# A float32 output projection whose late half becomes three products of rounded parts, in a fused two-block decoder layer stack on one core

## The reference, cut to what matters

```python
# first block, mixer 1
x = x + jnp.concatenate([y_a, y_b], axis=-1) @ w_out[l]
h = rms_norm(x, ffn_norm_g[l]).reshape(Bsz * S, D)
x = x + hier_moe(h, ...)
# second block, layer 0 (mixer 2) and layer 1 (HGRN2)
oa = rms_norm_2(oa, ret_g) * jax.nn.silu(heads(ag, RET_HEADS))
o = jnp.concatenate([oa.reshape(b, t, -1), ob.reshape(b, t, -1)], axis=-1)
h = h + o.astype(h.dtype) @ w_out          # 256 x 1024 times 1024 x 1024
h = h + swiglu(rms_norm_2(h, norm_ffn_g[l]), ...)
...
o = rms_norm_2(o, norm_g) * jax.nn.silu(heads(g))
h = h + o.reshape(b, t, d) @ w_out
h = h + moe_swiglu(rms_norm_2(h, norm_ffn_g[l]), ...)
```

## Time and profile before

| | |
|---|---|
| median of 3 runs (lowest, highest) | 2070.43 us (2069.76, 2073.31) |
| the profiled execution: its time, its span | 2070.48 us, 2068.7 us |
| TensorE busy, weight loads | 93% of the span, 58% |
| VectorE, ScalarE, GpSimd busy | 31%, 22%, 3% |
| chain that ended last, by engine | TensorE 70%, DMA 19%, VectorE 7%, ScalarE 2% |
| DMA | 653.16 MB, 316 GB/s over the span, 420 to 425 GB/s in the mixtures |
| float32 late and early halves of the projections (line 771) | 87.9 us, 3% of the chain |

### The profile page before, as it was taken

One profiled execution on the slowest core, in us unless ns is written; L12 is line 12 of the kernel. 1 busy time (PEld: TensorE's weight loads), 2 busy tenths in 40 slices (PEclk: granted clock), 3 DMA queues, 4 the chain that ended last, 5 costly groups with the idle time before them and its releaser, 6 DMA issues.

```text
span 2068.7 us, 38186 instructions
## 1 busy us (share of the span) xinstructions
PE 1923.2 (93%) x16861; PEld 1204.1 (58%) x16861; DVE 642.0 (31%) x1167; ACT 465.3 (22%) x652; POOL 70.1 (3%) x30
## 2 busy tenths in 40 slices
PE   9989978677887999999999999999999998999997
PEld 8988634343433898999999864433333433333433
DVE  4872311111111973644585640010010010010011
ACT  4621201100111553543465320100000010000011
POOL 5420000000000000000000000000000000000000
PEclk9999988988888999999999999999999999999999
DMA  8253699999999641555643358999999999999996
GB/s 321 100 204 122 267 422 424 425 425 422 425 424 392 234 149 35 163 186 191 236 161 125 123 200 344 388 422 420 421 420 420 420 419 422 420 421 417 409 419 270
DMA packets 126704, 653.16 MB, mean 316 GB/s; under 512 B 8928, under 2 KB 31584, under 8 KB 81376
## 3 DMA queue, kind: packets, MB, share of 16 engines
q1 hardware_dynamic: 126560, 650.98, 78.4%
HBM read 649.90 MB, written 1.05 MB: 315 GB/s over the span
## 4 chain that ended last, share of the span: by engine, by line
PE 70%; DMA 19%; DVE 7%; ACT 2%; issue 1%; SPq 0%; DVEq 0%; ACTq 0%
PE psum L2152 18%; DMA ring<-in_w_gate 15%; PE psum L2217 7%; PE psum L2158 6%; PE psum L579 5%; PE psum L581 5%; PE psum L580 5%; PE psum L1761 4%; PE psum L771 3%; PE psum L2222 3%; DMA ring<-in_moe_w_gate 2%; PE psum L2524 2%; DMA ring<-in_moe_w_down 1%; DVE arena L1219 1%; PE psum L628 1%
## 5 line engine op out<-in xcount | busy, mean ns | idle before, releaser
L2152 PE MATMUL psum<-ring,arena 128*32 128x384 f32 (+1 forms) x3584 | 366.8, 540 | 3.0 <-DMA ring<-in_moe_w_gate 1.8
L581 PE MATMUL psum<-ring_r 128*128 128x256 f32 x944 | 266.6, 282 | 0.0
L2152 PEld LDWEIGHTS psum<-ring,arena 128*32 128x32 f32 x3584 | 117.2, 110 | 214.9 <-issue 209.6
L1761 PE MATMUL psum<-ring,arena 128*32 128x512 f32 x896 | 153.6, 755 | 60.2 <-DMA ring<-in_w_gate 59.0
L2217 PE MATMUL psum<-ring,arena 128*32 128x512 f32 x1600 | 198.2, 594 | 9.5 <-DMA ring<-in_moe_w_down 9.4
L581 PEld LDWEIGHTS psum<-ring_r 128*128 128x128 f32 x944 | 180.4, 191 | 0.0
L579 PE MATMUL psum<-ring_r 128*128 128x256 f32 x608 | 176.8, 291 | 2.7 <-DVE ring_r L659 2.6
L580 PE MATMUL psum<-ring_r 128*128 128x256 f32 x608 | 172.7, 284 | 0.0
L2398 DVE TENSOR_TENSOR arena<-arena,psum 128x512 f32<-128x512 f32 (+1 forms) x42 | 23.7, 617 | 384.0 <-issue 348.0
L1761 PEld LDWEIGHTS psum<-ring,arena 128*32 128x32 f32 x896 | 39.8, 134 | 167.3 <-issue 167.3
L2158 PE MATMUL psum<-ring,arena 128*32 128x512 f32 (+1 forms) x1120 | 131.6, 539 | 0.0
(11 more groups left out here) (462 smaller groups left out, 2802.3 us busy)
## 6 DMA issues: line engine op xcount, KB each, us to landing
ring<-in_w_gate SPq DMA_DIRECT2D x64, 1024.0 KB, 21.7
ring<-in_moe_w_gate SPq DMA_DIRECT2D x64, 1024.0 KB, 20.1
ring<-in_moe_w_down SPq DMA_DIRECT2D x32, 2048.0 KB, 20.1
ring<-in_w_up SPq DMA_DIRECT2D x48, 1024.0 KB, 25.4
ring<-in_w_down SPq DMA_DIRECT2D x24, 2048.0 KB, 25.7
ring<-in_moe_w_up SPq DMA_DIRECT2D x48, 1024.0 KB, 20.8
ring<-in_moe_w_gate SPq DMA_DIRECT2D x64, 768.0 KB, 18.5
ring<-in_moe_w_up SPq DMA_DIRECT2D x48, 768.0 KB, 18.4
```

The lines of the kernel that those rows point to most:

```text
L581: return nc.tensor.matmul(out, al, bh, start=False, stop=stop, **kw)
L1761: mm = nc.tensor.matmul(bank(0)[s * C:(s + 1) * C, :], q_Xg[:, k * PC + x * C:k * PC + (x + 1) * C], w[s][:, k, :], start=(k == 0), stop=( ...
L2152: mm = nc.tensor.matmul(bank(b0 + j)[n * MORE:(n + 1) * MORE, 0:Q], z_Xg[:, x:x + MORE], w[:, (2 * h + j) * Q:(2 * h + j + 1) * Q], start= ...
```

## The change

- `late_products` takes the place of the late blocks. A quarter is 16 products of the rounded and the remainder weights by the rounded `y` and then 8 of the rounded weights by the remainder of `y`: 24 fp32r products for 8 float32 ones. The first 16 wait for the rounded `y` and the remainder weights of quarter 0, quarter 1 for the other remainder weights.
- ScalarE rounds the late four chunks of the output weight into slot 6, quarter by quarter (`out_weights_hi`, four activations of 128 x 1024 for each projection), after the last input projection has been through that slot. VectorE writes the remainders over the weights (`out_weights_lo`, four subtractions).
- `split_y` makes `y` in two parts in slot 5: rounded, full, remainder. The gate is multiplied in ahead of the wait for rstd.
- In HGRN2 the warm-up in front of the late half is 9 matmuls, not 12.
- Since slots 5 and 6 stay in use until the end of the projection, up 0 and down 1 of moe1 are sent after it. For moe2 `SLOT_ORDER` puts slot 4 ahead of slot 6; chunk 7 alone is sent after the last input projection, chunks 8, 9, 10 after quarter 1 and chunks 6, 11, 12, 13 after quarter 3.

```diff
-SLOT_ORDER = (1, 2, 3, 5, 6, 4, 0)
+SLOT_ORDER = (1, 2, 3, 5, 4, 6, 0)
...
+        def out_weights_hi(act, st, part, tag, last, late, quarters=range(4)):
+            act.wait_ge(*E[st].at(f"{last}_q3"))
+            for r in quarters:
+                w, landed_sem, value = piece(part, f"{tag}_{r // 2}")
+                act.wait_ge(landed_sem, value)
+                nc.scalar.activation(out_hi[st][:, r], late_columns(w, late, r), ACT.Copy).then_inc(*S[st].step())
...
+        def split_y(dve, st, y, rstd, hi, lo, name):
+            v = V[st]
+            nc.vector.tensor_tensor(hi, y, rstd, ALU.mult).then_inc(*v.step())
+            v.name(f"{name}_hi")
+            nc.vector.tensor_tensor(y, y, rstd, ALU.mult).then_inc(*v.step())
+            dve.wait_ge(*v.last())
+            nc.vector.tensor_tensor(lo, y, hi.bitcast(F32), ALU.subtract).then_inc(*v.step())
+            v.name(f"{name}_lo")
...
+            def late_products(self, r, late, tokens, first):
+                for b in (2 * r, 2 * r + 1):
...
+                    for k in range(4):
+                        for w in (out_hi[self.st][:, r, b % 2, k, :], lo[:, k, :])[0:2 if first else 1]:
+                            mm = nc.tensor.matmul(bank(r)[:, (b % 2) * T:(b % 2 + 1) * T], w, tokens[:, k, :],
+                                                  start=False, stop=(not first and k == 3), skip_group_check=True)
...
-                self.pe.wait_ge(*ready)
-                for b in range(8):
-                    mm = self.block(b, late, False)
...
+                self.pe.wait_ge(*V[self.st].at(f"{self.tag}_lo0"))
+                self.pe.wait_ge(*y_hi)
+                for r in range(4):
+                    if r == 1:
+                        self.pe.wait_ge(*V[self.st].at(f"{self.tag}_lo3"))
+                    self.late_products(r, late, hi, True)
+                    if r == 0:
+                        self.pe.wait_ge(*y_lo)
+                    self.late_products(r, late, lo, False).then_inc(*E[self.st].step())
...
+                    if r:
+                        following(r - 1)
...
-            out.finish(v.at("h1y"), lambda r: route_quarter(pe, M2, r), warm=12)
+            out.finish(v.at("h1y1_hi"), v.at("h1y1_lo"), lambda r: route_quarter(pe, M2, r), warm=9)
...
+            sp.wait_ge(*piece_used("hg1"))
+            moe2_load(0, 7)
+            sp.wait_ge(*E["hgrn"].at("out3_0_1"))
+            for at in (8, 9, 10):
+                moe2_load(0, at)
+            sp.wait_ge(*E["hgrn"].at("out3_1_1"))
+            for at in (6, 11, 12, 13):
+                moe2_load(0, at)
```

More of the change, by code:

```diff
@@ L410, in _ @@
             send_down(one(0), 0)
[L411 to L414, removed]
+            sp.wait_ge(*piece_used(last_in("one", 2)))
+            for half in range(2):
+                send_ups(one(2), half, 0, 1)
+            sp.wait_ge(*piece_used(last_in("one", 3)))
+            for half in range(2):
+                send_ups(one(0), half, 0, 0)
+            send_down(one(1), 2)
+            for half in range(2):
+                send_ups(one(3), half, 1, 1)
             sp.wait_ge(*V["route1"].at("trips"))
@@ L1135, in mixer1_scalar @@
             s.name("wT")
+            out_weights_hi(act, st, "one", "out1", "z", 4)
             act.wait_ge(*e.at(f"o{NCH - 1}"))
@@ L1360, in mixer1_vector @@
                     dve.wait_ge(*v.last())
-            dve.wait_ge(*s.at("o_rstd"))
[L1363 to L1367, removed]
+            out_weights_lo(dve, st, "one", "out1", 4, range(4))
+            dve.wait_ge(*s.at("o_sq"))
+            yb = m1_ycat[:, HC:2 * HC]
+            nc.vector.scalar_tensor_tensor(yb, bank(6, 2), param("dn_g"), m1_sz, ALU.mult, ALU.mult).then_inc(*v.step())
+            dve.wait_ge(*v.last())
+            dve.wait_ge(*s.at("o_rstd"))
+            split_y(dve, st, yb, m1_X, yh_r, yl_r, "y")
             M1.router_times_gamma(dve)
@@ L2727, in attend_tensor, with attend_vector @@
             sums(1)
-        def attend_vector(dve, x, decay, meanwhile=None, between=lambda c: None):
+        def attend_vector(dve, x, decay, meanwhile=None, between=lambda c: None, last=False):
             e, s, v, tag = E[x.st], S[x.st], V[x.st], x.tag
@@ L2748, in attend_vector @@
                 meanwhile()
+            if last:
+                for t in range(NT):
+                    y = by_time(x.y, t)
+                    dve.wait_ge(*s.at(f"{tag}osq{t}"))
+                    dve.wait_ge(*s.at(tag + "gate"))
+                    nc.vector.scalar_tensor_tensor(y, bank_heads(6 + t), x.gain, by_time(x.gate, t), ALU.mult, ALU.mult)\
+                        .then_inc(*v.step())
+                    dve.wait_ge(*v.last())
+                    dve.wait_ge(*s.at(f"{tag}orstd{t}"))
+                    split_y(dve, x.st, y, by_time(c_AT, t), by_time(yh_r, t), by_time(yl_r, t), f"{tag}y{t}")
+                v.name(tag + "y")
+                return
             for t in range(NT):
@@ L2918, in mixer2_tensor @@
             attend_tensor(pe, RET, out, (1, 1, 1, 0, 1))
-            out.finish(v.at("ay"), lambda r: norm_tensor(pe, "ffn", r))
+            out.finish(v.at("ay1_hi"), v.at("ay1_lo"), lambda r: norm_tensor(pe, "ffn", r))
         def mixer2_scalar(act, waits):
@@ L3001, in mixer2_scalar @@
             keep("ag", halves(a_gate), parts=(1,))
+            out_weights_hi(act, st, "two", "out2", "ag", 0, (0, 1))
             for b in range(2):
@@ L3010, in mixer2_scalar @@
             s.name("akd")
+            out_weights_hi(act, st, "two", "out2", "ag", 0, (2, 3))
             act.wait_ge(*s.at("ag_1"))
@@ L3142, in mixer2_vector @@
             v.name("aqd")
-            attend_vector(dve, RET, lambda h, c: CHUNK_DECAY[h])
+            out2_lo = ((0, 1), (), (2, 3))
+            attend_vector(dve, RET, lambda h, c: CHUNK_DECAY[h],
+                          between=lambda c: out_weights_lo(dve, st, "two", "out2", 0, out2_lo[c]), last=True)
             for n in range(2):
@@ L3626, in hgrn_vector @@
                 gated_vector_round(dve, HG[1], n)
-            attend_vector(dve, HG[1], decay)
+            attend_vector(dve, HG[1], decay,
+                          between=lambda c: out_weights_lo(dve, st, "two", "out3", 4, range(4) if c == 2 else ()),
+                          last=True)
             M2.router_times_gamma(dve)
```

41 lines of the change are left out of this document (27 added, 14 removed).

## The result

The changed kernel takes 2075.47 us in the median of 20 runs (2072.53 to 2080.61), the kernel before 2071.97 in 20 runs beside it (2069.76 to 2074.90): a ratio of 1.0017, 95% interval 1.0011 to 1.0023. The forecast was 2064.5, range 2061.5 to 2070.5. So the change costs some 3.5 us where 6 were to be saved. The profiled execution took 2073.07 us, with a span of 2071.2, 2.5 above the span of before. What follows is read from these two executions and so accounts for 2.5 of the 3.5 us.

The account below looks back on a forecast made before the run. Mixtures bound by DMA (moe2 also TensorE) end as much earlier as they start; stretches between are TensorE's. Savings 2.3 + 0.6 + 3.1 = 6.0 us off 2070.48 give 2064.5; own range 2061.5 to 2066.5, 8 in 10 2061.5 to 2070.5.

Parts of the forecast that it names:

- The price of a quarter: Late output projections: 24 fp32r products at 0.120 us replace 16 instructions at 0.216, 3.45 to 2.88 us, 0.57 saved.
- rival 2: Late quarters: weight loads of 0.19 us not overlapped, so 24 products take 4.6 us; 2082.4 us in all, chance 0.04.
- Mixer 1, "I cost these at nothing": Mixer 1's weight rounding and subtractions fit engine waiting time, y is not waited for, so 2.3 us are saved.
- Mixer 2: Mixer 2's projection: residual sum waits for ffn weight remainders, so net only 0.6 us saved (ends 0.4 and 1.1).
- The stand of 2.1 us before the norm: Mixer 2: TensorE idles 2.1 us before quarter 0's norm matmul, which comes 0.5 later, at 828.5.
- If one overruns it costs 0.1 us: Mixer 2: added roundings and subtractions fit narrowly in ScalarE's 2.05 and VectorE's 2.46 us gaps; an overrun costs 0.1 us.
- HGRN2: Last mixer's projection: late half starts 0.8 us earlier and four quarters save 2.3, together 3.1 us.
- The held-back loads: Moved moe1 and moe2 loads land before the first buffer release, margins 6 and 1 us, so nothing is lost.
- Rival 1: Prefetch late at the first release, costing up to 9.9 us in moe1 and 7.5 in moe2: 2081.9 us, chance 0.08.
- 1.3 us to start: Held-back loads: 1.3 us allowed for the first load to start, in the landing times 221.1 (moe1) and 1223.0 (moe2).
- side estimate: Before moe2: at the skill's 358 GB/s limit chunks would land at 1227, costing some 2 us; not charged.
- Rival 3: VectorE replaces TensorE at more ends than mixer 2, or the clock halves (3.4 us): about 2067.7 us, chance 0.22.

Follow-up runs that it names:

- e4: The kernel before with only mixer 1's output projection and the moe1 loads changed: 2077.17 us, ratio 1.0019.
- e1: The kernel before with seven one-element VectorE memsets added at the end of mixer 1, nothing of the change: 2078.51 us against 2072.60, ratio 1.0033.
- e2: The changed kernel with VectorE's final_g scalings moved behind the z bias and bv's remainders: 2069.86 us, ratio to the kernel before 0.9987.
- e9: The changed kernel with SyncE holding the load of av until mixer 2's softplus is done: 2075.89 us, ratio to the kernel before 1.0018.
- e5: The kernel before with only mixer 2's output projection changed, all loads as before: 2073.63 us, ratio 1.0007.
- e7: The changed kernel with final_g scalings behind the z bias, mixer 2's weights rounded after the decayed keys, residual sums between feed-forward remainders: 2065.66 us, ratio to before 0.9970.
- e3: The kernel before with only the last mixer's output projection and the moe2 loads changed: 2068.90 us, ratio 0.9982.

## Why the prediction was wrong, point by point

- **The price of a quarter** was right: 3.13 us for a train of 24 with its last end, so 0.12 a product, and rival 2 (weight loads set the pace) is out.
- **Mixer 1, "I cost these at nothing"** is the step that failed. The cover was there, as forecast: the late half waits for neither weights nor `y`, and moe1 starts 2.66 us earlier against 2.3. But the four subtractions and the three-step `y` were priced by their duration alone. As instructions they also moved the border of VectorE's code by seven places in the program, 500 us further on, from where nobody waits to just ahead of bv's remainders. That cost 5.2 us in the changed kernel, 5.2 in e4, and 5.4 with seven empty instructions in e1. That the border had lain well in before was luck: no part of the working looked at it.
- **Mixer 2** was forecast at -0.6 and lost 2.1 from the mask on (228.2 against 226.1). The stand of 2.1 us before the norm came as forecast and is paid for in the -0.6. "If one overruns it costs 0.1 us" was mis-sized: ScalarE began 1.83 us late, and TensorE waited 0.95. The half clock behind the stand (0.72 over 831 to 836) was left out of the sum; its 3.41 us cost about 1.7, an estimate at half speed. With -0.5 these make the 2.1. An instruction packet runs just where ScalarE stands (796.47 to 797.02), so this may be ScalarE's code. For it: e2 and e9 stand at the same place (1.78 and 2.03 us), as in the changed kernel behind 459 of ScalarE's records and 1.0 to 1.2 us after a packet, and e5, with five records fewer ahead of its roundings, does not. No run was made to test it. Alone, without ScalarE's stand, the part gave -0.5 (e5), and with both repairs -2.7 (e7), of the 2.3 us that four quarters of products can give and what the sums' order adds.
- **HGRN2** was right: 3.0 against 3.1. In e3 the last two stages are 2.5 us shorter and the median 3.7, in a kernel whose clock stays whole in mixer 3, as in before.
- **The held-back loads** were right. The DMA engines were busy until about the first release of moe2, as the thin margin of 1 us had it, and moe2 got no longer (857.6 against 859.2). Rival 1 is out. The forecast's 1.3 us to start is not in its rows; in the changed kernel the first packets ahead of moe2 move 0.95 us after the issue (1204.71 and 1205.66). Its side estimate, chunks in at 1227, lies 3.1 us behind the 1223.9 and not some 2; the sum did not use it.
- **Rival 3** had a new VectorE wait and a half clock take the gain, and both happened, at more than twice its price. The half clock behind mixer 2's stand is one that it named; the wait at bv's remainders and the half clock there, the larger loss, are not. No rival slower than before rested on VectorE.

The Trainium skill (Runtime: NRT & Kernel Launch, Instruction fetch mechanics) says that an engine's instructions come in blocks of 16 KiB, 256 instructions, each fetched while the one before runs, so that a border is mostly hidden. The trace does not agree for this border: 2.5 to 3.25 us in the open in six kernels. The same section of the Trainium skill warns that a taken branch can force such a fetch. VectorE leaves the loop of moe1 ahead of this place, but no run here shows whether that is why.

## What to carry to other kernels

Count instructions, not only their time: here seven more on VectorE shifted the place where, as far as the runs tell, its code is loaded, and that cost 5 us, some 500 us behind the edit. When an engine stands and the named semaphore was already given, look for an instruction packet in the DMA view, and test by adding a few empty instructions to the old kernel. If it is so, put work that nobody waits for at the border, as e2 did, before giving up the change.

## What the runs showed of the hardware that was not expected

- What the count marks as a border of VectorE's code stood in the open for 2.5 to 3.25 us in six kernels, of which 1.34 to 1.56 passed after the packet had ended. It held to the same count, 742 records of this trace, in all ten kernels in which VectorE stood.
- The stand's follow-up cost another 2.2 to 2.5 us: TensorE sat idle for 4.0 to 4.8 us, and its clock was at the half level for 6.8 us in each of the six kernels with that stand, beginning 1.1 to 1.8 us before TensorE went on.
- An idle DMA system brought the code hardly earlier: the packet came 25.96 us after the end of the first sum of moe1's last round in e9, 26.36 in the changed kernel.
